# High weights against both parts of the activations in one 512-column matmul, and PSUM tiles left in two units

## The chip, the cores and the metric

The kernel runs on one core of a Trainium2 chip. The metric is the device time of one execution in microseconds (us); the figure for a kernel is the median over its runs. The engines are TensorE (PE; its weight loads are listed as PEld), VectorE (DVE), ScalarE (ACT), GpSimd (POOL) and SyncE (SP, which issues the DMAs).

## The reference, cut to what matters

The reference computes two transformer-like layers on 256 tokens with width 2048, in float32: adaLN modulation, gated linear attention, latent attention, a SwiGLU feed-forward part of hidden width 5632, then pooling, memory attention, compressed and windowed sparse attention, and RMS norms between them. Nearly all of the arithmetic is products of the 256 activations' rows with weight matrices:

```python
p = h @ w_in                      # 2048 x (many parts)
y_gla = o @ gla_wo ; y_mla = o_m @ mla_wo
merged = sigmoid(p_ga) * y_gla + sigmoid(p_gb) * y_mla ; x = x + gate_m * (merged @ w_out)
g, u = split(h @ ffn_w_in) ; x = x + gate_f * ((silu(g) * u) @ ffn_w_down)
# second layer: pool_u, pool_zu, nsa_k*, nsa_q, nsa_zq ... and two output products
```

## The kernel before, in words

**A split product.** Both factors are float32, and both are cut in two float32r parts: hi is the value as float32r holds it, lo is what is left. A product is hi·hi + hi·lo + lo·hi. The activations lie in SBUF with features on the partitions (h_hi, h_lo and the like: 128 partitions, 16 chunks, 256 tokens).

**Pieces and tiles.** A product (class `Product`, table `PRODUCTS`, L133 to L194) is a row of tiles, each 512 output features wide, and a tile is a row of kp pieces (kp is 4 for most, 6 and 5 in the two ffn_down products). A piece is 4 chunks of 128 input features by 512 output features, 1 MB, brought by one DMA into one of four buffers w_raw. Then ACT writes w_hi in two halves of 128x1024 (L1242), DVE writes w_lo in two halves (L1555); w_hi and w_lo have two buffers each, so the cut of piece n+2 waits until PE is done with piece n (semaphore piece_done).

**PE.** In `product` (L837 to L891) each piece waits for its w_lo; then, for each chunk, three passes (w_hi with x_hi, w_lo with x_hi, w_hi with x_lo) over four blocks of 128 output features: 48 matmuls of 256 columns, each with its own weight load. A few products have the weights as the moving operand instead (mode "N", 512 columns, gla_v for one; mode "R" for cmp_k1 and cmp_v1, where three matmuls in a row add into the same PSUM columns). A tile's sums, 4 blocks of 256 columns, fill one of the two buffers tile_ps[0], tile_ps[1] (two PSUM banks each), and the tiles take turns.

**Leaving PSUM.** After the last piece of a tile, one engine takes the whole tile of 128x1024: ACT with a copy, sigmoid or silu (`copy_to` L1285, `silu_g` L1455, `silu_gate` L1485) or DVE (`gated` L1910 to L1916, `gla_merge` L1924, `both_merge` L1950 to L1952, `add` in `residual` L1973 and L1977, `up` L1999 to L2005). In the program of ACT and of DVE (L1255 to L1271 and L1571 to L1590) the order is: the cuts up to the first piece of the next tile, with the steps of `between` after each of them, then the take of the tile, then the cut of the next tile's second piece. That last cut can begin only when the tile is done, so it lies behind the take, on both engines, while PE runs one piece. The PE waits again at that next tile's second piece.

**Other work on the same engines.** Products with a rider carry the adaLN product: after every second piece an extra 1 MB lands in w_raw, which DVE multiplies and adds in four steps of 128x512 (`ada_piece`, L1605, L1612), and PE sums it (`ada_total`, L893). `between` weaves in rotations, the log-sigmoid of gla_k (L1423 to L1425), the high part of z (L1511) and attention steps. `residual` products that feed a norm also square x on ACT (L1348) and, from the second tile on, reduce the squares on DVE (L1966).

**Loops.** `turns` (L625) makes a hardware loop of two tiles per turn for gate_a, gla_wo, mla_wo and the ffn_in products (L600 to L621 hold the waits with a loop count in them); the other split products are written out flat.

## Time and profile before

| | |
|---|---|
| median of 3 runs (lowest, highest) | 3026.41 us (3026.32, 3032.33) |
| the profiled execution | 3026.54 us, of it the span of the instructions 3024.7 us |
| PE busy / weight loads busy | 2817.4 us (93%) / 2703.1 us (89%) |
| DVE busy / ACT busy | 1830.7 us (61%) / 1195.1 us (40%) |
| mean granted TensorE clock | 0.969 |
| HBM read | 561.95 MB, 187 GB/s over the span |

The busy time of PE is the union of its matmuls, which overlap; the distance between two starts is what a matmul costs in a stream. A timeline row gives the start, the time until the end of the last of its instructions, the group and its count; in brackets stands the idle time before it and what ended it.

### The profile page before, as it was taken

To read this page: it belongs to the slowest core of one execution; us is meant where nothing else is said; L and a number is where in the kernel's file an instruction comes from. 1 tells how busy PE (TensorE), PEld (TensorE's weight loads), DVE (VectorE), ACT (ScalarE), POOL (GpSimd) and SP (SyncE) were. 2 spreads that over 40 slices of the span, in tenths; PEclk is the share of its full clock that TensorE was granted. 3 is DMA by queue.
4 is the path that set the end of the run, shared out by engine and by line. 5 is a ranking of instruction groups with operands and counts; after the bars stand their busy time and mean duration, and the time that the engine had idled before them with its cause. 6 is when DMAs were issued, how large, how long until landed. Compare 5 with 4: busy or idle time off the path is not lost.

```text
span 3024.7 us, 50507 instructions
## 1 busy us (share of the span) xinstructions
PE 2817.4 (93%) x21461; PEld 2703.1 (89%) x21461; DVE 1830.7 (61%) x2283; ACT 1195.1 (40%) x1508; POOL 5.6 (0%) x14
## 2 busy tenths in 40 slices
PE   3879988999999999989999999998998989899998
PEld 2879867999999779989999999997998989799887
DVE  7795666867665557774444444455566656646765
ACT  3435433343343433343333333333444434544543
POOL 0000000000000000000000000000000000000000
PEclk7989999999999989999999999999999999999998
DMA  7786831777777337745555555553554445665232
GB/s 266 280 313 220 288 111 70 257 258 274 250 241 216 91 109 254 265 166 194 180 180 181 181 181 181 180 180 125 168 181 157 162 148 181 199 184 164 87 106 88
DMA packets 319760, 568.44 MB, mean 188 GB/s; under 512 B 21962, under 2 KB 61218, under 8 KB 318963
## 3 DMA queue, kind: packets, MB, share of 16 engines
q1 hardware_dynamic: 318354, 561.73, 55.5%
q0 software_dynamic: 1248, 4.46, 0.4%
q8 instruction: 118, 1.93, 0.3%
q14 instruction: 40, 0.32, 0.0%
HBM read 561.95 MB, written 4.19 MB: 187 GB/s over the span
## 4 chain that ended last, share of the span: by engine, by line
PE 83%; DVE 12%; issue 2%; ACT 2%; DMA 1%; SPq 0%; DVEq 0%; ACTq 0%
PE tile_ps L835 75%; PE misc_ps L835 6%; DVE w_lo L1555 4%; DVE probs_t L1612 1%; ACT w_hi L1242 1%; PE misc_ps L977 1%; DVE rstd L1662 0%; DVE o_tmp L1999 0%; DVE x L1977 0%; DVE tile_ps L1895 0%; DVE gla_att L1898 0%; DMA w_raw<-in_w_mem_kv 0%; PE tile_ps L1017 0%; DVE stats L1774 0%; DMA mem_rows<-in_mem 0%
## 5 line engine op out<-in xcount | busy, mean ns | idle before, releaser
L1555 DVE TENSOR_TENSOR w_lo<-w_raw,w_hi 128x1024 fp32r<-128x1024 f32 x866 | 1021.8, 1222 | 885.5 <-ACT w_hi L1242 884.5
L1242 ACT ACTIVATE w_hi<-w_raw 128x1024 fp32r<-128x1024 f32 x866 | 867.9, 1050 | 1128.0 <-PE tile_ps L835 1086.5
L835 PE MATMUL tile_ps<-h_hi,w_hi 128*128 128x256 f32 x4208 | 697.0, 287 | 55.6 <-DVE w_lo L1555 34.6
L835 PE MATMUL tile_ps<-h_hi,w_lo 128*128 128x256 f32 x4208 | 687.0, 285 | 0.0
L835 PE MATMUL tile_ps<-h_lo,w_hi 128*128 128x256 f32 x4208 | 686.9, 285 | 0.0
L835 PEld LDWEIGHTS tile_ps<-h_hi,w_hi 128*128 128x128 f32 x4208 | 590.7, 194 | 65.3 <-issue 34.9
L835 PEld LDWEIGHTS tile_ps<-h_hi,w_lo 128*128 128x128 f32 x4208 | 587.9, 194 | 0.0
L835 PEld LDWEIGHTS tile_ps<-h_lo,w_hi 128*128 128x128 f32 x4208 | 587.7, 194 | 0.0
L1612 DVE SCALAR_TENSOR_TENSOR probs_t<-w_raw,c_act,probs_t 128x512 f32<-128x512 f32 x360 | 270.3, 751 | 10.9
L835 PE MATMUL tile_ps<-o_hi,w_hi 128*128 128x256 f32 x1024 | 168.4, 287 | 14.4 <-DVE o_lo L1648 6.9
L835 PE MATMUL tile_ps<-o_hi,w_lo 128*128 128x256 f32 x1024 | 165.9, 285 | 0.0
L835 PE MATMUL tile_ps<-o_lo,w_hi 128*128 128x256 f32 x1024 | 165.5, 284 | 0.0
L835 PEld LDWEIGHTS tile_ps<-o_hi,w_hi 128*128 128x128 f32 x1024 | 142.7, 194 | 16.3 <-issue 11.4
L835 PEld LDWEIGHTS tile_ps<-o_hi,w_lo 128*128 128x128 f32 x1024 | 142.6, 194 | 0.0
L835 PEld LDWEIGHTS tile_ps<-o_lo,w_hi 128*128 128x128 f32 x1024 | 142.2, 193 | 0.0
L835 PE MATMUL tile_ps<-sw_hi,w_hi 128*128 128x256 f32 x704 | 113.8, 284 | 1.7 <-DVE w_lo L1555 1.5
L835 PE MATMUL tile_ps<-sw_hi,w_lo 128*128 128x256 f32 x704 | 113.3, 283 | 0.0
L835 PE MATMUL tile_ps<-sw_lo,w_hi 128*128 128x256 f32 x704 | 113.3, 283 | 0.0
L835 PEld LDWEIGHTS tile_ps<-sw_hi,w_hi 128*128 128x128 f32 x704 | 97.1, 192 | 2.7 <-DVE w_lo L1555 2.7
L835 PEld LDWEIGHTS tile_ps<-sw_lo,w_hi 128*128 128x128 f32 x704 | 97.2, 192 | 0.0
L835 PEld LDWEIGHTS tile_ps<-sw_hi,w_lo 128*128 128x128 f32 x704 | 97.2, 192 | 0.0
L835 PE MATMUL tile_ps<-w_hi,h_hi 128*128 128x512 f32 x224 | 70.7, 397 | 0.0
(330 smaller groups left out, 2281.3 us busy)
## 6 DMA issues: line engine op xcount, KB each, us to landing
w_raw<-in_ada_w SPq DMA_DIRECT2D x96, 1024.0 KB, 5.2
w_raw<-in_w_in SPq DMA_DIRECT2D x89, 1024.0 KB, 5.1
w_raw<-in_ffn_w_in SPq DMA_DIRECT2D x88, 1024.0 KB, 5.0
w_raw<-in_w_out SPq DMA_DIRECT2D x48, 1024.0 KB, 5.1
w_raw<-in_ffn_w_down SPq DMA_DIRECT2D x44, 1024.0 KB, 5.1
w_raw<-in_b_w_in SPq DMA_DIRECT2D x33, 1024.0 KB, 5.3
w_raw<-in_a_w_in SPq DMA_DIRECT2D x32, 1024.0 KB, 5.6
w_raw<-in_w_kv SPq DMA_DIRECT2D x24, 1024.0 KB, 5.1
```

The source lines that it names most:

```text
L835: return nc.tensor.matmul(o, l, r, start=start, stop=stop, skip_group_check=True)
L977: last = nc.tensor.transpose(bank[2][0:k, a * P:(a + 1) * P], probs_of(name, u0 + e)[:, hd * nk + j * P:hd * nk + j * P + k], ident)
L1242: f(w_hi[s_ % 2][:, hf], w_raw[r % 4][:, hf], ACT.Copy).then_inc(cut_hi, 1)
L1555: ins = v.tensor_tensor(w_lo[s_ % 2][:, hf], w_raw[r % 4][:, hf], f32(w_hi[s_ % 2][:, hf]), ALU.subtract)
L1612: ins = v.scalar_tensor_tensor(acc, w[:, c, :], c_act[:, k:k + 1], acc, ALU.mult, ALU.add)
```

## The change

- `Product.paired` holds for split products of mode "T" with at least four pieces per tile, other than pool_out, nsa_out, mem_k0, mem_k1, nsa_qm and nsa_zm. Such a tile is two units (nu = 2) of two blocks of 128 output features. A unit has its own tile_ps buffer: each block fills one bank of 512 columns.
- The hi and lo part of an activation lie in one tensor (h_2, o_2, cq_2, ckv_2, sw_2). For each chunk and block PE runs one matmul of 512 columns, w_hi with the 256 columns of x_hi and the 256 of x_lo, and one of 256 columns, w_lo with x_hi, into the first half of the same bank. A piece runs unit 0's four chunks, then unit 1's. The first tile after a norm (`by_chunk`) goes chunk by chunk instead, except in its last piece.
- Unit 0 is done half a piece before the tile (semaphore half_done). Where `folds` holds (all paired products but w_out, ffn_down0, ffn_down1), each unit leaves PSUM so: ACT copies the second halves of both banks (128x512) into `folded`, a part of probs_t; DVE adds the first halves and frees the PSUM buffer; the former take follows, at 128x512, from SBUF; it raises `made`, and the next unit's ACT copy waits for it, since there is one `folded`.
- The residual products add the two halves to x one after the other on DVE, eight steps of 128x256 for a tile where there were four.
- In ACT's and DVE's programs a `between` step that followed the cut of the next tile's first piece now follows the two takes.
- The two accumulators of the adaLN product become one in mla_ckv (`ada_turns`).

The core of the diff:

```diff
+        self.paired = kp >= 4 and split and mode == "T" and not late and name not in ONE_BY_ONE
+        self.folds = self.paired and name not in RESIDUAL
+        self.nu = 2 if self.paired else 1
...
-        h_hi = at("h_hi", HB, [P, DC, S], F32R)
-        h_lo = at("h_lo", HB + 16 * KB, [P, DC, S], F32R)
+        h_2 = at("h_2", HB, [P, 2, DC, S], F32R)
+        h_hi, h_lo = h_2[:, 0], h_2[:, 1]
...
+        folded = probs_t[:, 1, :].rearrange("p (a n) -> p a n", a=2)
...
+        def sums_from(ps, h):
+
+            return ps[:].rearrange("p (a b n) -> p b a n", a=2, b=2)[:, h]
...
+                        def two_blocks(u, c):
                             k = q * g.kc + c
...
+                            ps = psum_unit(g, g.nu * tb + u)[0]
+                            for j in range(2):
+                                at_ = slice((2 * u + j) * P, (2 * u + j + 1) * P)
+                                mm(ps[:, j * 512:j * 512 + 512], w[0][:, c, at_], x_2(tb, k), k == 0, False)
+                                last = mm(ps[:, j * 512:j * 512 + S], w[1][:, c, at_], x_hi(tb, k), False,
+                                          k == g.kp * g.kc - 1)
+                            return last
...
+                        elif g.paired:
+                            for u in range(2):
+                                unit_is_free(u)
+                                for c in range(g.kc):
+                                    if u == 0:
+                                        chunk_is_there(c)
+                                    last = two_blocks(u, c)
+                                if u == 0 and q == g.kp - 1:
+                                    last.then_inc(half_done, 1)
...
-                                do_next(between)
-                        if take:
-                            ps, tk = psum_tile(g, tb)
-                            tile_is_done(act, g, i, tb)
-                            take(i, tb, g, ps, tk)
+                                if not (g.paired and e == g.done_at[tb]):
+                                    do_next(between)
+                        for u in range(g.nu * tb, g.nu * tb + g.nu):
+                            ps, tk = psum_unit(g, u)
+                            if g.folds:
+                                low_part(i, u, g, ps)
+                            if take:
+                                unit_is_there(act, g, i, u)
+                                take(i, u, g, ps, tk)
+                        if g.paired:
+                            do_next(between)
+
+            def low_part(i, u, g, ps):
+
+                unit_is_done(act, g, i, u)
+                unit_is_made(act, g, i, u - 1)
+                f(folded, sums_from(ps, 1), ACT.Copy).then_inc(low_out, 1)
...
+            def fold(i, u, g, ps, tk):
+
+                dve.wait_ge(low_out, g.f0 + u + 1 + per(i, g.body * g.nu))
+                v.tensor_tensor(folded, sums_from(ps, 0), folded, ALU.add).then_inc(tk, 1)
...
-            def both_merge(i, tb, g, ps, tk):
-                tile_is_done(dve, g, i, tb)
-                last_taken(dve, g, i, tb)
-                t = in_chunks(mla_tmp[:])
-                step(i, tb, g, 0, v.tensor_tensor(t, in_chunks(ps[:]), some(gate_b, i, tb, g), ALU.mult))
-                step(i, tb, g, 1, v.tensor_tensor(t, t, some(merged, i, tb, g), ALU.add))
-                split_to(i, tb, g, 2, t, some(h_hi, i, tb, g), some(h_lo, i, tb, g), tk)
+            def both_merge(i, u, g, ps, tk):
+                unit_is_taken(dve, g, i, u)
+                step(i, u, g, 0, v.tensor_tensor(folded, folded, some(gate_b, i, u, g), ALU.mult))
+                step(i, u, g, 1, v.tensor_tensor(folded, folded, some(merged, i, u, g), ALU.add))
+                split_to(i, u, g, 2, folded, some(h_hi, i, u, g), some(h_lo, i, u, g), made)
...
-                    for c in range(BLK):
-                        cc = (i * g.body + tb) * BLK + c
-                        ins = v.scalar_tensor_tensor(x[:, cc, :], ps[:, c * S:(c + 1) * S], mod[:, part * DC + cc:part * DC + cc + 1],
-                                                     x[:, cc, :], ALU.mult, ALU.add)
+                    for h in range(2):
+                        for c in range(2):
+                            cc = (i * g.body * 2 + u) * 2 + c
+                            ins = v.scalar_tensor_tensor(x[:, cc, :], sums_from(ps, h)[:, c, :], mod[:, gate * DC + cc:gate * DC + cc + 1],
+                                                         x[:, cc, :], ALU.mult, ALU.add)
+                        if h == 0:
+                            own.wait(ins)
...
-                t = o_tmp[:, 0, :]
...
-                v.tensor_tensor(t, ps[:], t, ALU.mult).then_inc(tile_step, 1)
...
+                unit_is_taken(dve, g, i, u)
+                silu = in_pair(o_tmp[:, 0, u % 2 * 512:u % 2 * 512 + 512])
+                m = u // 4 * 2 + u % 2
+                step(i, m, g, 0, v.tensor_tensor(folded, folded, silu, ALU.mult))
+                at_ = bass.ds(per(i, g.body * 2) + 2 * m, 2)
+                split_to(i, m, g, 1, folded, sw_hi[:, at_, :], sw_lo[:, at_, :], made)
```

## Rows read from the trace of the kernel before

**Rows 1.** The page: busy time of each engine.

```profile
PE 2817.4 (93%) x21461; PEld 2703.1 (89%) x21461; DVE 1830.7 (61%) x2283; ACT 1195.1 (40%) x1508; POOL 5.6 (0%) x14
```

**Rows 2.** The page: the chain that ended last, by engine and by line.

```profile
PE 83%; DVE 12%; issue 2%; ACT 2%; DMA 1%; SPq 0%; DVEq 0%; ACTq 0%
PE tile_ps L835 75%; PE misc_ps L835 6%; DVE w_lo L1555 4%; DVE probs_t L1612 1%; ACT w_hi L1242 1%; PE misc_ps L977 1%; DVE rstd L1662 0%; DVE o_tmp L1999 0%; DVE x L1977 0%; DVE tile_ps L1895 0%; DVE gla_att L1898 0%; DMA w_raw<-in_w_mem_kv 0%; PE tile_ps L1017 0%; DVE stats L1774 0%; DMA mem_rows<-in_mem 0%
```

**Rows 3.** Waits, whole span: in total us, times, longest us.

```profile
PE tile_ps L835 <- DVE w_lo L1555: 54.7, 28, 15.4
```

**Rows 4.** Busy time by stretch: gate_a (a rider), and pool_zu to pool_zm.

```profile
604.00:698.90 94.90, 94.70 (x788) 94.09 (x786) 63.29 (x67) 41.14 (x40) 0.00 (x0) 1.00 0.76 266
2190.00:2305.00 115.00, 115.00 (x961) 115.00 (x960) 63.72 (x57) 48.69 (x47) 0.00 (x0) 1.00 0.52 167
```

**Rows 5.** Timeline of PE, ffn_in0: start us, us, group.

```profile
1500.40 0.64 PE L835 MATMUL tile_ps<-h_hi,w_lo 128*128 128x256 f32 x4
1500.88 0.64 PE L835 MATMUL tile_ps<-h_lo,w_hi 128*128 128x256 f32 x4
```

**Rows 6.** Timeline of PE, gla_v: matmuls of 512 columns.

```profile
340.36 0.61 PE L835 MATMUL tile_ps<-w_hi,h_hi 128*128 128x512 f32 x2
340.81 0.62 PE L835 MATMUL tile_ps<-w_lo,h_hi 128*128 128x512 f32 x2
```

**Rows 7.** Timeline of PE, cmp_k1: each adds into the same PSUM columns.

```profile
2594.12 0.28 PE L835 MATMUL tile_ps<-w_lo,z_hi 128*60 128x256 f32 x1
2594.24 0.28 PE L835 MATMUL tile_ps<-w_hi,z_lo 128*60 128x256 f32 x1
```

**Rows 8.** Timeline of ACT and DVE at a tile's end in ffn_in0, silu tile.

```profile
1346.64 1.03 ACT L1485 ACTIVATE o_tmp<-tile_ps 128x1024 f32<-128x1024 f32 x1 [2.39 <-PE tile_ps L835]
1347.56 1.99 ACT L1242 ACTIVATE w_hi<-w_raw 128x1024 fp32r<-128x1024 f32 x2
1348.64 2.36 DVE L1555 TENSOR_TENSOR w_lo<-w_raw,w_hi 128x1024 fp32r<-128x1024 f32 x2 [4.18 <-ACT w_hi L1242]
```

**Rows 9.** Timeline at a tile's end in ffn_down1: DVE's cut and PE's wait.

```profile
2005.15 2.36 DVE L1555 TENSOR_TENSOR w_lo<-w_raw,w_hi 128x1024 fp32r<-128x1024 f32 x2 [2.14 <-ACT w_hi L1242]
2006.43 0.64 PE L835 MATMUL tile_ps<-sw_lo,w_hi 128*128 128x256 f32 x4
2007.57 0.39 PE L835 MATMUL tile_ps<-sw_hi,w_hi 128*128 128x256 f32 x1 [0.49 <-DVE w_lo L1555]
```

**Rows 10.** Groups by form: operations of 128x512 (and 128x256 for L1977).

```profile
L1363 ACT ACTIVATE probs_t<-misc_ps 128x512 f32<-128x512 f32 x28 | 16.7, 597 | 59.7 <-PE misc_ps L977 59.7
L1770 DVE SCALAR_TENSOR_TENSOR probs<-misc_ps,const 128x512 f32<-128x512 f32 x6 | 4.1, 686 | 6.0 <-PE misc_ps L835 4.9 <-PE misc_ps L977 1.1
L1977 DVE SCALAR_TENSOR_TENSOR x<-tile_ps,mod,x 128x256 f32<-128x256 f32 x48 | 19.9, 478 | 27.2 <-PE tile_ps L835 27.2
```

**Rows 11.** Timeline of DVE, the looped up tile of ffn_in0.

```profile
1415.92 1.23 DVE L1999 TENSOR_TENSOR o_tmp<-tile_ps,o_tmp 128x1024 f32<-128x1024 f32 x1 [2.40 <-PE tile_ps L835]
1417.31 0.69 DVE L2003 CAST sw_hi<-o_tmp 128x1024 f32 x1 [0.16 <-DVE o_tmp L1999]
1419.27 2.35 DVE L1555 TENSOR_TENSOR w_lo<-w_raw,w_hi 128x1024 fp32r<-128x1024 f32 x2
```

**Rows 12.** PE's waits in two windows: gla_g (527:604), mla_wo (1112:1212.9).

```profile
PE tile_ps L835 <- DVE w_lo L1555: 1.9, 2, 0.9
...
PE tile_ps L835 <- DVE w_lo L1555: 3.8, 3, 1.6
```

**Rows 13.** Timeline of ACT: a table load in gate_a, the log-sigmoid of gla_k.

```profile
284.47 0.58 ACT L1423 ACTIVATE log_a<-misc_ps 128x512 f32<-128x512 f32 x1
288.31 0.63 ACT L1425 ACTIVATE log_a<-log_a 128x512 f32<-128x512 f32 x1
...
628.37 1.28 ACT L1285 ACT_TABLE_LOAD   x1 [3.83 <-PE tile_ps L835]
```

**Rows 14.** Groups by form: the high part of z.

```profile
L1511 ACT ACTIVATE z_hi<-z_pe 128x1920 fp32r<-128x1920 f32 x2 | 3.6, 1794 | 0.0
```

More of the change, by code:

```diff
@@ L130, in constants @@
     return c, g.reshape(P, GLA_CONST_W)
+RESIDUAL = ("w_out", "ffn_down0", "ffn_down1")
+ONE_BY_ONE = ("mem_k0", "mem_k1", "nsa_qm", "nsa_zm")
 class Product:
@@ L220 @@
         _s += _g.tiles * _g.kp * _g.split
-        _t += _g.tiles
+        _t += _g.tiles * _g.nu
+        _f += _g.tiles * _g.nu * _g.folds
+        _h += _g.tiles * _g.paired
     _a += _g.ada_tiles(_g.tiles)
@@ L251 @@
     _k += _g.sums != "shared"
-    _a += {"pairs": _g.n // 2, "tiles": 4, "shared": 0, "heads": GLA_H}[_g.sums]
+    _a += {"pairs": _g.n // 2, "tiles": 4 * _g.nu, "shared": 0, "heads": GLA_H}[_g.sums]
     _m += {"pairs": _g.n // 2, "tiles": 1, "shared": 0, "heads": 1}[_g.sums]
@@ L601, in all_taken @@
         def all_taken(eng, g):
+            if g.folds:
+                eng.wait_ge(made, g.f0 + g.tiles * g.nu)
+                return
             for b in range(2):
@@ new lines, in unit_is_free, with chunk_is_there @@
+                        def unit_is_free(u):
+                            use = (g.t0 + g.nu * tb + u) // 2
+                            if use and q == 0:
+                                pe.wait_ge(psum_unit(g, g.nu * tb + u)[1], use + per(i, g.body * g.nu // 2))
+                        def chunk_is_there(c):
+                            if tb == 0 and chunk_ready:
+                                for sem_, v_ in chunk_ready(q * g.kc + c):
+                                    pe.wait_ge(sem_, v_)
@@ L1117, in _ @@
             product("gate_a", *h)
-            for b in range(2):
-                pe.wait_ge(taken[b], (G["gla_g"].t1 - b + 1) // 2)
+            all_taken(pe, G["gla_g"])
             product("gla_wo", *o)
@@ L1459, in _ @@
             product("gla_wo")
[L1460 to L1461 removed]
+            product("mla_cq", copy_to(chunks(cq), pre=[(piece_done, G["gla_wo"].p1)]))
+            product("mla_ckv", copy_to(chunks(ckv)))
             all_taken(act, G["mla_cq"])
             norm("cq")
[L1464 removed]
+            product("mla_kr", copy_to(lambda i, u, g: k_rope[:, :]))
             all_taken(act, G["mla_ckv"])
             norm("ckv")
[L1467 removed]
+            product("gate_b", copy_to(chunks(gate_b), ACT.Sigmoid, pre=[(made, G["gla_g"].f0 + G["gla_g"].tiles * 2)]), flat=True)
             for hf in range(2):
                 free = [(piece_done, G["gate_b"].p1)] if hf == 0 else [(at_o, U0["mla0"] + len(UNITS["mla0"]))]
[L1470 to L1473 removed]
+                product(f"mla_qn{hf}", copy_to(chunks(mla_q), pre=free))
+                product(f"mla_qr{hf}", copy_to(chunks(mla_qr)))
+                product(f"mla_k{hf}", copy_to(chunks(mla_k)))
+                product(f"mla_v{hf}", copy_to(columns(mla_v)))
                 attention(f"mla{hf}")
@@ L1479, in silu_gate, with take @@
             def silu_gate(part):
-                def take(i, tb, g, ps, tk):
-                    if tb % 2:
-                        return
-                    act.wait_ge(taken[(g.t0 + 1) % 2], (g.t0 + 1 + tb) // 2 + per(i, g.body // 2))
-                    f(o_tmp[:, 0, :], ps[:], ACT.Silu).then_inc(tk, 1)
+                def take(i, u, g, ps, tk):
+                    if u // 2 % 2 == 0:
+                        f(in_pair(o_tmp[:, 0, u % 2 * 512:u % 2 * 512 + 512]), folded, ACT.Silu).then_inc(made, 1)
                 return take
@@ L1586, in product @@
                                     cut(g, i, g.s0 + e, g.p0 + e, ring_of(g, e))
-                                do_next(between)
-                        if take:
-                            ps, tk = psum_tile(g, tb)
-                            take(i, tb, g, ps, tk)
+                                if not (g.paired and e == g.done_at[tb]):
+                                    do_next(between)
+                        for u in range(g.nu * tb, g.nu * tb + g.nu):
+                            ps, tk = psum_unit(g, u)
+                            if g.folds:
+                                fold(i, u, g, ps, tk)
+                            if take:
+                                take(i, u, g, ps, tk)
+                        if g.paired:
+                            do_next(between)
+            def fold(i, u, g, ps, tk):
+                dve.wait_ge(low_out, g.f0 + u + 1 + per(i, g.body * g.nu))
+                v.tensor_tensor(folded, sums_from(ps, 0), folded, ALU.add).then_inc(tk, 1)
             def ada_piece(g, i, tb, q):
```

309 lines of the change are left out of this document (160 added, 149 removed).

## The prediction

> **What bounds the kernel now.** First the busy times: PE works 93% of the span, its weight loads 89%, DVE 61%, ACT 40% [rows 1]. Then the chain that ended last: 83% of it is PE, 75% the split products; the only other entry of size is DVE's w_lo with 4% [rows 2]. The waits say the same: PE stands 54.7 us in all for w_lo, in 28 places [rows 3]. The busy times by stretch show how full PE is: in pool_zu to pool_zm it never idles, 961 matmuls in 115.0 us, 0.120 us each; in gate_a it nearly never does, with the DMA engines at 0.76 and 266 GB/s [rows 4]. So a gain must come from PE's stream, and a loss from what ends after PE: the second piece of a tile, whose w_lo lies behind the taking of the tile before.
>
> **PE's stream.** Two groups of four 256-column matmuls start 0.48 us apart, 0.120 each [rows 5]; two groups of two 512-column matmuls 0.45 to 0.46, 0.227 each over a stretch (1340.36 to 1344.44 in such rows is 18 matmuls in 4.08 us) [rows 6]. So 256 columns more cost 0.107, and each matmul has a fixed 0.013 with its weight load. Before, a chunk and block cost 3 x 0.120 = 0.360; after, 0.227 + 0.120 = 0.347. The columns streamed, 768, stay; only one fixed part goes. A piece of 16 such pairs goes from 5.76 to 5.55, 0.208 less. Paired are 78 tiles: 70 of 4 pieces, 4 of 6 and 4 of 5, which is 324 pieces: **-67.4 us** in all. Nine of these pieces start a stage and last as long as a norm or the attention before them: +1.9.
>
> The trace has no 512 beside a 256 and none whose moving operand is two runs of 256. In cmp_k1 matmuls of 256 columns that add into the same PSUM columns start 0.12 apart [rows 7], so adding to what was just written costs nothing. Bounds for the pair: 0.321 (columns alone, 3 x 0.107) and 0.360 (the fixed part comes back). I take 0.347, the sum of the two nearest rows.
>
> The Trainium skill, "TensorE: Matmul & The Clock Gate", section "Wait — 56ns, not 53.3ns?", gives N/2.4 GHz plus about 2.5 ns between matmuls, 216 ns for 512 columns, and has weight loads run ahead. By it the pair would be about 325 ns and the saving 180 us by an estimate. The rows here show 227 and 120, so the trace disagrees.
>
> **The drain.** PE loses time at a tile's second piece when w_lo's second half ends later than 0.32 before the end of the running piece: in ffn_down1 it ends at 2007.51, 0.44 after the piece (2006.43 + 0.64), PE restarts at 2007.57, and an unhindered stream would have restarted 0.16 before the piece's end, with 0.11 for refilling [rows 9]. I count T from the tile's end on PE; the next piece then has until T + 5.76 - 0.32 = 5.44 before, T + 5.23 after.
>
> Before, an ACT tile: copy starts at T+0.04, w_hi 0.92 later, first half 1.05, w_lo 0.03 later, 2.36 for both halves: 4.4 [rows 8]. No loss.
>
> After, unit 1 is the one that counts. Operations at 128x512: ACT 0.60, DVE 0.69 [rows 10]. Handovers between engines are 0.03 to 0.09 in flat code [rows 8], 0.16 in loops [rows 11].
> - **ACT tile, flat** (28: gla_q, gla_k, mla_cq, mla_ckv, gate_b, pool_u to pool_zm, nsa_kc, vc, ks, kw, q, zq): 0.07 + 0.60 + 0.03 + 0.69 + 0.06 + 0.53 (copy until w_hi may start) + 1.05 + 0.03 + 2.36 = 5.42, loss 0.2: +5.6. Unit 0 costs nothing: its sums are there at T-2.7, DVE is through with its w_lo at T-2.0, so it is folded by T-1.3. If that cover is gone, its 1.9 us join the 5.42.
> - **gate_a** (4, loop): 5.6, loss 0.4. Before, two loop turns lost some 0.3 per tile behind a table load of 1.28 [rows 13], which now falls beside unit 0: +1.
> - **gla_wo** (4): take is one multiply, ACT cuts meanwhile: w_lo ends at 4.6, no loss.
> - **ffn_in** (11 pairs of silu and up tile, loop): the silu tile loses 0.4. In the up tile DVE folds, multiplies, casts (0.43, an estimate from 0.69 at 1024) and subtracts: 0.84 + 0.84 + 0.56 + 0.60 = 2.84. Unit 0 starts it at T-2.0 and is made at T+1.0; only then may ACT copy unit 1: 1.1 to 1.7, fold at 1.8, w_lo starts at 4.6 and ends at 7.0. Loss 1.75. Before, w_lo ended at 1419.27 + 2.35, with DVE's take from 1415.92 on [rows 11]: loss 0.4. Difference 1.75: +19.3. That is all the 18.3 that their 88 pieces save.
> - **mla_wo** (4, loop): one operation more per unit: unit 0 is made at T+1.8, w_lo ends at 8.6, loss 3.4; before 1.8 (idle 1.6 and refill) [rows 12]: +6.4.
> - **gla_g** (4, flat): two steps of 0.48, multiply, cast, subtract: made at T+1.5, w_lo ends at 7.8, loss 2.6; before 1.2 [rows 12]: +5.6.
> - **w_out, ffn_down** (12): four steps of 0.478 [rows 10] and one wait more for unit 1 (1.9 against 1.7), a square of half the size on ACT: the loss of 0.76 in w_out and ffn_down1 grows by 0.1, ffn_down0 loses nothing: +0.6.
> - **between moved behind the takes.** DVE's steps lie beside ACT's copy and w_hi: nothing. ACT's do not: one log-sigmoid of gla_k, 4.5 us from 284.47 to 288.94 [rows 13], makes that loss 4.7, with a window of 1.2 gone elsewhere, and the other three windows stay bound by ACT: +4.1. The high part of z in nsa_ks, 1.79 [rows 14]: +1.9.
> - **Stage ends.** Where a later stage waits for the last unit, 1.0 later, mostly hidden: +1.5. The riders' adaLN steps on DVE end just in time before their piece's w_lo; SP's DMAs are the same in number and order, and 266 GB/s becomes 276: nothing. The queues that wait behind `made` are ACT's cuts, counted above. POOL has no step in it.
>
> **Sum:** -67.4 + 1.9 + 5.6 + 1 + 19.3 + 6.4 + 5.6 + 0.6 + 4.1 + 1.9 + 1.5 = **-19.5 us**. The profiled execution took 3026.5 (span 3024.7), the median is 3026.4: **3007 us**.
>
> **The rivals.**
> 1. *The drain is longer than I count* (slower). Place: the handovers ACT, DVE, ACT of unit 1 between T and the next w_lo. Price: 78 tiles; 0.25 us more in each and no gain is left. If every flat handover costs the loop's 0.16 to 0.24, five of them add 0.6 in some 40 flat tiles (24 us) and 0.3 in the others (11 us): 3042. For: five steps follow one another with nothing beside them. Against: the flat rows agree on 0.03 to 0.09.
> 2. *The pair costs 0.360*: the second run of the operand, or the change of length, brings the 0.013 back. Drains stay at +48: 3074. For: no row shows such an operand. Against: the fixed part is the same at 256 and 512.
> 3. *Columns alone count*: if the fixed part comes from a weight load that the 256-column stream is too short for, the 512 makes room, and the pair costs 0.321. Then a piece is 5.14, the pieces save 201 us, and the drains lose 0.4 more in some 60 tiles: about 2898. Against: 512 in a row cost 0.227, not 0.214 [rows 6]. The rule of the Trainium skill's "TensorE: Matmul & The Clock Gate" quoted above leads here.
> 4. *Nothing of note*: drains eat the saving to within the measurement. It is the upper part of my own case.
>
> **How the numbers follow.** What a measurement of this kernel can tell from no change is 0.2%, 6 us. My case has 0.75: 2985 to 3025, of it 0.66 faster, 0.09 same. Rival 1 has 0.15 (0.12 slower, 0.03 same), rival 2 0.05, rival 3 0.03, and 0.02 for no change at all. Together faster 0.69, same 0.14, slower 0.17. The range that leaves out 2 in 10 goes from 2980 (ACT and DVE steps overlap more than counted) to 3038.
>
> **What would show it.** In the changed profile the 512- and 256-column matmuls should start 0.347 us apart per pair and a flat stretch such as pool_zu should take 5.55 per piece; PE's waits for w_lo should grow from 54.7 to some 90 us, most of it in ffn_in and mla_wo, at second pieces; in an up tile ACT's copy of unit 1 should start about 1 us after T. The prediction is wrong if pairs start 0.36 or 0.32 apart, if ffn_in's stretch of 12 tiles changes by more than 5 us, or if flat ACT tiles lose more than 0.5 each.

## The result, and the profile after

The changed kernel took 3039.88 us (median of 20 runs, 3030.86 to 3051.89), the kernel before, on the same chip, 3028.3 us (20 runs, 3022.92 to 3032.4). The ratio is 1.0042, 95% interval 1.0032 to 1.0053: **slower by 0.4%**, where 0.6% faster was forecast. The profiled execution of the changed kernel took 3051.07 us (span 3049.3), one of its longest.

The page of the changed kernel: busy times, the chain by engine and by line, and three groups (the drain's two new operations and the 512-column matmuls; the number behind the bar is busy us and mean ns, then the idle time before).

```profile
PE 2806.6 (92%) x16277; PEld 2439.1 (80%) x16277; DVE 1950.0 (64%) x2528; ACT 1286.1 (42%) x1695; POOL 5.6 (0%) x14
...
PE 79%; DVE 13%; ACT 3%; issue 3%; DMA 1%; SPq 0%; DVEq 0%; ACTq 0%
...
L878 PE MATMUL tile_ps<-h,w_hi 128*128 128x512 f32 (+1 forms) x4448 | 1502.8, 391 | 79.1 <-DVE w_lo L1644 47.9
...
L1690 DVE TENSOR_TENSOR probs_t<-tile_ps,probs_t 128x512 f32<-128x512 f32 x132 | 91.2, 691 | 114.3 <-ACT probs_t L1360 112.2
...
L1360 ACT ACTIVATE probs_t<-tile_ps 128x512 f32<-128x512 f32 x132 | 79.1, 599 | 152.8 <-PE tile_ps L878 97.1
```

There are 5184 matmuls fewer than in [rows 1], yet PE is busy only 10.8 us less, and PE's share of the chain is 79% where [rows 2] had 83%. The stream did become cheaper; the time came back as waits, and as PE time at half clock. The waits of PE, whole span (us in total, times, longest):

```profile
PE tile_ps L878 <- DVE w_lo L1644: 69.2, 37, 15.4
...
PE tile_ps L878 <- issue: 15.8, 7, 4.2
```

The first row answers to [rows 3]. The second is new: five of its seven waits stand at tile starts of ffn_in0 (below).

**Where it went, product by product.** The table sets the time from the end of one product to the end of the next, read off PE's last matmuls in both traces, against the prediction's terms shared out over the products (0.208 us per piece, and the drain's terms).

| product | pieces | forecast, us | measured, us |
|---|---|---|---|
| gla_k (log-sigmoids moved) | 8 | +2.8 | +2.4 |
| gla_g | 16 | +2.3 | +7.9 |
| gate_a | 16 | -2.3 | +2.7 |
| gla_wo | 16 | -3.3 | -3.4 |
| mla_cq, mla_ckv, mla_kr | 8 | at most +0.2 | +4.7 |
| mla_qn0, mla_qn1 (attention beside them) | 0 | 0 | +11.9 |
| mla_wo | 16 | +3.1 | +4.5 |
| w_out | 16 | -3.1 | +0.1 |
| ffn_in0 | 48 | +0.5 | +8.6 |
| ffn_in1 | 40 | +0.4 | -0.1 |
| ffn_down0, ffn_down1 | 44 | -8.9 | -3.4 |
| pool_u to pool_zm | 32 | -5.1 | -2.6 |
| nsa_kc to nsa_kw | 16 | -0.6 | -0.5 |
| nsa_q, nsa_zq | 24 | -3.8 | -4.1 |

The measured column, with gla_q, gate_b and what little lies in the rest, makes the 24.6 us between the two spans. Five things carry the miss: ffn_in0, the attention stage, a group of products with one or two pieces of 9.2 to 9.7 us (gla_g, gate_a, mla_wo, w_out), mla_kr, and a stream that in most pieces is slower than forecast, which shows best in the ffn_down products, where little else changed. The busy times of four stretches, after (the stretch and its length, busy us and instructions of PE, PEld, DVE, ACT and POOL, then the granted clock, the DMA share and GB/s, as in [rows 4]):

```profile
401.90:611.20 209.30, 181.63 (x964) 147.33 (x962) 146.28 (x167) 70.63 (x75) 0.00 (x0) 0.94 0.34 121
...
846.10:860.40 14.30, 11.19 (x63) 10.15 (x63) 6.76 (x12) 6.98 (x12) 0.00 (x0) 0.76 0.44 159
...
1335.20:1636.20 301.00, 281.42 (x1558) 242.34 (x1559) 167.65 (x191) 128.66 (x152) 0.00 (x0) 0.97 0.48 167
1773.10:2004.90 231.80, 227.80 (x1281) 196.04 (x1281) 124.51 (x129) 97.60 (x109) 0.00 (x0) 1.00 0.53 181
```

These are gla_g, mla_kr, ffn_in0 and ffn_in1. In ffn_in0 PE idles 19.6 us, in ffn_in1, which does the same work on ten tiles, only 4.0.

**The stream.** PE's 512-column matmuls after, one pair with its neighbour in pool_zu:

```profile
2231.11 0.40 PE L878 MATMUL tile_ps<-h,w_hi 128*128 128x512 f32 x1
2231.35 0.28 PE L878 MATMUL tile_ps<-h,w_lo 128*128 128x256 f32 x1
2231.46 0.40 PE L878 MATMUL tile_ps<-h,w_hi 128*128 128x512 f32 x1
```

The 512 takes 0.24, the 256 behind it 0.11. Over longer stretches there are two rates: in gla_wo 17 pairs in 5.89 us (729.95 to 735.84), 0.347 each as forecast; in ffn_in1 15 pairs in 5.30 us (1818.27 to 1823.57), 0.353. A piece is so 5.55 or 5.65; of the 324 pieces 94 have the first, 143 the second, and 12 lie between 5.70 and 5.80. A piece keeps the rate of the one before it as long as nothing is waited for: among neighbours at one of the two rates it is the same in 150 of 152 cases.

**The drain, as it was counted.** ffn_in1, silu and up tile: what ACT and DVE do around the end of an up tile, and where PE restarts.

```profile
1819.23 0.60 ACT L1360 ACTIVATE probs_t<-tile_ps 128x512 f32<-128x512 f32 x1 [2.90 <-DVE sw L1750]
...
1819.86 0.69 DVE L1690 TENSOR_TENSOR probs_t<-tile_ps,probs_t 128x512 f32<-128x512 f32 x1 [0.67 <-ACT probs_t L1360]
...
1820.66 0.69 DVE L2099 TENSOR_TENSOR probs_t<-probs_t,o_tmp 128x512 f32<-128x512 f32 x1
...
1821.51 0.43 DVE L1749 CAST sw<-probs_t 128x512 f32 x1 [0.16 <-DVE probs_t L2099]
...
1822.08 0.69 DVE L1750 TENSOR_TENSOR sw<-probs_t,sw 128x512 f32 x1
...
1822.69 2.35 DVE L1644 TENSOR_TENSOR w_lo<-w_raw,w_hi 128x1024 fp32r<-128x1024 f32 x2
...
1825.10 0.51 PE L878 MATMUL tile_ps<-h,w_hi 128*128 128x512 f32 x1 [1.01 <-DVE w_lo L1644]
```

The first row waits 2.90 us for unit 0 to be made (the one buffer folded), and unit 1's four operations then follow one another on DVE. The second piece of the tile that follows an up tile takes 6.91 to 6.93, a loss of 1.26, where 1.75 was forecast.

**ffn_in0.** The same operations around 1395.8, where an up tile ends:

```profile
1393.65 0.69 DVE L1690 TENSOR_TENSOR probs_t<-tile_ps,probs_t 128x512 f32<-128x512 f32 x1
...
1395.56 0.69 DVE L1750 TENSOR_TENSOR sw<-probs_t,sw 128x512 fp32r<-128x512 f32 x1
...
1396.37 0.60 ACT L1360 ACTIVATE probs_t<-tile_ps 128x512 f32<-128x512 f32 x1 [2.75 <-DVE sw L1750]
...
1397.00 0.69 DVE L1690 TENSOR_TENSOR probs_t<-tile_ps,probs_t 128x512 f32<-128x512 f32 x1 [0.74 <-ACT probs_t L1360]
...
1397.79 0.47 PE L878 MATMUL tile_ps<-h,w_hi 128*128 128x512 f32 x1 [2.00 <-issue]
```

Here PE doesn't start the next silu tile at 1395.8. It stands 2.00 us, until 0.10 after unit 1 of the tile before has been folded. The page puts that down to "issue", but five such restarts, at 1397.79, 1446.74, 1494.11, 1543.09 and 1590.62, all come right behind a fold. The reason is in the program: `by_chunk` asks for both units' PSUM before the first chunk, in every tile with tb == 0, and in a hardware loop of two tiles per turn that is the first tile of every turn, not of the product alone. Unit 1's bank is then wanted as soon as PE ends the tile before, half a piece earlier than otherwise.

**The clock.** Windows over the 4 us behind three of the waits: one in gla_g (1.94 us before it), the first and the second of ffn_in0 (2.00 and 2.22 us before them):

```profile
541.50:545.50 4.00, 3.89 (x13) 3.36 (x14) 3.89 (x6) 0.28 (x1) 0.00 (x0) 0.57 0.67 217
1397.50:1401.50 4.00, 3.71 (x13) 3.19 (x14) 3.90 (x6) 2.00 (x2) 0.00 (x0) 0.61 0.13 51
...
1446.50:1450.50 4.00, 3.76 (x21) 3.33 (x22) 3.67 (x6) 2.01 (x2) 0.00 (x0) 1.00 0.05 17
```

In the first two PE issues 13 matmuls where it issues 21 in the third: the granted clock went from 2.4 to 1.2 GHz behind the wait. A piece of ffn_in0 that starts so takes 9.36 or 9.55, one that starts behind as long a wait at full clock 8.01 to 8.16: **1.2 to 1.5 us more**, on top of the wait. Beside gla_k's piece of 10.45, which waits for a log-sigmoid, ten paired pieces of the changed kernel take 9.16 to 10.51 us (three in gla_g, two in mla_wo and in ffn_in0, one each in gate_a, gate_b and w_out); the kernel before has two (10.14 in gla_g, 9.73 in gate_b). Summed from the clock's records between 100 and 2900 us of the span, it stands at 1.2 GHz for 201 us after and for 126 us before. Time and clock go together in the other runs as well: of the changed kernel's 20 runs the fastest (3030.86 us) has a mean clock of 0.964, the slowest (3051.89) 0.957.

**mla_kr.** ACT and DVE at the end of mla_ckv:

```profile
844.48 0.57 ACT L1360 ACTIVATE probs_t<-tile_ps 128x512 f32<-128x512 f32 x1
845.93 0.69 DVE L1690 TENSOR_TENSOR probs_t<-tile_ps,probs_t 128x512 f32<-128x512 f32 x1
...
846.65 0.63 ACT L1369 ACTIVATE ckv<-probs_t 128x512 f32<-128x512 f32 x1 [1.60 <-DVE probs_t L1690]
...
847.37 0.60 ACT L1360 ACTIVATE probs_t<-tile_ps 128x512 f32<-128x512 f32 x1
848.00 0.69 DVE L1690 TENSOR_TENSOR probs_t<-tile_ps,probs_t 128x512 f32<-128x512 f32 x1 [1.39 <-ACT probs_t L1360]
848.73 0.63 ACT L1369 ACTIVATE ckv<-probs_t 128x512 f32<-128x512 f32 x1 [0.76 <-DVE probs_t L1690]
849.26 1.13 ACT L1399 ACTIVATE nscratch_o<-cq 128x512 f32<-128x512 f32 x2
...
849.93 3.78 PE L878 MATMUL misc_ps<-nscratch_o,const 128*128 128x256 f32 x8 [3.07 <-ACT nscratch_o L1399]
```

The same sums in the kernel before:

```profile
841.42 2.00 PE L835 MATMUL misc_ps<-nscratch_o,const 128*128 128x256 f32 x8 [0.85 <-ACT nscratch_o L1307]
```

Unit 0's fold sits behind DVE's w_lo, unit 1's copy behind unit 0; ACT's program has the squares of cq, which were ready long before, behind all this. PE waits 3.07 us for them (before: 0.85), and its eight sums then take 3.78 us instead of 2.00, at half clock; over the stretch the mean clock is 0.76, where it was 1.00. Of the 4.9 us that mla_kr is longer 2.2 are so the wait and 1.8 the clock behind it.

### The profile page after: what moved, and what is told of

The parts are those of the page before. It is cut to its first block, busy times and chain, and to the rows that moved or that the text cites. A ratio compares the mean times of both kernels' runs of the same rounds, so it can differ in the third digit from the quotient of the medians.

```text
span 3049.3 us, 40930 instructions
## 1 busy us (share of the span) xinstructions
PE 2806.6 (92%) x16277; PEld 2439.1 (80%) x16277; DVE 1950.0 (64%) x2528; ACT 1286.1 (42%) x1695; POOL 5.6 (0%) x14
## 4 chain that ended last, share of the span: by engine, by line
PE 79%; DVE 13%; ACT 3%; issue 3%; DMA 1%; SPq 0%; DVEq 0%; ACTq 0%
PE tile_ps L878 72%; PE misc_ps L878 6%; DVE w_lo L1644 4%; DVE probs_t L1712 2%; ACT w_hi L1319 1%; DVE probs_t L1690 1%; ACT probs_t L1360 1%; PE misc_ps L1054 1%; DVE rstd L1764 0%; DVE x L2079 0%; DVE tile_ps L1997 0%; DVE gla_att L2000 0%; DVE part_o L2067 0%; DMA w_raw<-in_w_mem_kv 0%; DVE probs_t L2099 0%
## 5 line engine op out<-in xcount | busy, mean ns | idle before, releaser
L878 PE MATMUL tile_ps<-h,w_hi 128*128 128x512 f32 (+1 forms) x4448 | 1502.8, 391 | 79.1 <-DVE w_lo L1644 47.9
L878 PE MATMUL tile_ps<-h,w_lo 128*128 128x256 f32 x4208 | 1165.8, 283 | 0.0
L878 PEld LDWEIGHTS tile_ps<-h,w_hi 128*128 128x128 f32 x4448 | 824.3, 191 | 275.8 <-DVE w_lo L1644 58.0
L878 PEld LDWEIGHTS tile_ps<-h,w_lo 128*128 128x128 f32 x4208 | 797.5, 192 | 0.6
L878 PE MATMUL tile_ps<-o,w_hi 128*128 128x256 f32 (+1 forms) x1536 | 333.6, 325 | 17.7 <-DVE w_lo L1644 8.7
L878 PEld LDWEIGHTS tile_ps<-o,w_hi 128*128 128x128 f32 x1536 | 232.8, 193 | 43.9 <-DVE w_lo L1644 10.6
L878 PE MATMUL tile_ps<-sw,w_hi 128*128 128x512 f32 x704 | 249.1, 399 | 3.4 <-DVE w_lo L1644 3.4
L878 PE MATMUL tile_ps<-o,w_lo 128*128 128x256 f32 x1024 | 227.5, 283 | 0.0
L878 PE MATMUL tile_ps<-sw,w_lo 128*128 128x256 f32 x704 | 197.4, 280 | 0.0
L878 PEld LDWEIGHTS tile_ps<-o,w_lo 128*128 128x128 f32 x1024 | 170.0, 193 | 0.0
L878 PEld LDWEIGHTS tile_ps<-sw,w_hi 128*128 128x128 f32 x704 | 132.2, 188 | 37.6 <-DVE w_lo L1644 5.0
```

The source lines that it names most:

```text
L878: return nc.tensor.matmul(o, l, r, start=start, stop=stop, skip_group_check=True)
```

## The experiments

Ratios are to the kernel before on the same chip, with 95% intervals. All start from the changed kernel. The lengths of stretches come from one profiled execution each.

**1. No chunk order in ffn_in0.**

```diff
-            product("ffn_in0", *h, chunk_ready=as_normed("ffn"), by_chunk=True)
+            product("ffn_in0", *h, chunk_ready=as_normed("ffn"))
```

> The changed kernel with by_chunk taken from ffn_in0 alone. In the trace of the changed kernel PE stands 2.0 to 2.3 us at the start of five silu tiles of ffn_in0, until the fold of the up tile's second unit is done, and never so in ffn_in1. Theory A: by_chunk holds in every turn of PE's loop, since the turn's first tile is tb 0, and it asks for both units at once. Then these five waits go, waits of about 1.0 for w_lo at the second piece take their place as in ffn_in1, ffn_in0 falls from 301 us to about 293, and the ratio to the kernel before falls from 1.0042 by about 0.003 to 1.001. Rival B: the waits come from the drain itself, one folded buffer and made; then they stay or move, ffn_in0 stays at 299 to 302 and the ratio at 1.004.

Measured: 3034.98 us, 1.0035 (1.0021 to 1.0049). ffn_in0:

```profile
1324.80:1617.30 292.50, 279.35 (x1558) 240.13 (x1559) 167.53 (x191) 128.65 (x152) 0.00 (x0) 0.98 0.51 172
```

292.5 where it was 301.0, PE idle 13.1 instead of 19.6; the five waits at tile starts are gone and second pieces of 6.6 to 7.0 stand in their place, as in ffn_in1. The clause that `by_chunk` gives every turn costs 8.5 us in this stretch; 6.5 of them are idle time, and most of the rest is the clock, which fell behind two of the five waits and behind none here. The ratio shows less of it than was expected: it fell by 0.0007, not by 0.003, and the two intervals overlap. The fastest run fell from 3030.86 to 3025.32 us and the slowest from 3051.89 to 3044.46, so the medians agree with a gain, but the 8.5 us rest on the two profiles.

**2. No low copy.** ACT's copy and DVE's fold are replaced by one DVE copy of the first halves: the sum of w_hi with x_lo, in the second halves, is left out of the output.

```diff
-                                low_part(i, u, g, ps)
...
-                v.tensor_tensor(folded, sums_from(ps, 0), folded, ALU.add).then_inc(tk, 1)
+                v.tensor_copy(folded, sums_from(ps, 0)).then_inc(tk, 1)
```

> The changed kernel without ACT's copy of the second halves: DVE copies the first halves to folded and no lo-part sum is added, so the product of w_hi with the activations' lo part is left out. The drain of each folding unit is shorter by one ACT step and one handover, 0.6 to 0.7 us. Theory A (the drain between a tile's end and the next w_lo sets the loss): waits of PE for w_lo at second pieces shrink by about 0.65 in each of the some 35 tiles that lose now, twice that in ffn_in's up tiles and mla_wo where unit 0 hands on to unit 1, some 30 to 40 us in all, ratio about 0.992. Rival B (the drain costs little, the loss lies in PE's stream or in the clock): ratio stays within 0.002 of 1.0042.

Measured: 3013.97 us, 0.9957 (0.9940 to 0.9974). gla_g took 203.9, gate_a 93.3, mla_wo 141.8, w_out 94.2 (its late pieces without a clock fall), ffn_in0 294.8, ffn_in1 227.3, mla_kr 12.5. So one more operation of 0.60 us and its handover in each unit's way costs some 26 us (1.0042 less 0.9957, times 3026; 30 to 40 had been expected), and without it the change would be faster than before.

**3. Order of the matmuls.** Two 512-column matmuls, then the two of 256.

```diff
                             for j in range(2):
                                 at_ = slice((2 * u + j) * P, (2 * u + j + 1) * P)
                                 mm(ps[:, j * 512:j * 512 + 512], w[0][:, c, at_], x_2(tb, k), k == 0, False)
+                            for j in range(2):
+                                at_ = slice((2 * u + j) * P, (2 * u + j + 1) * P)
                                 last = mm(ps[:, j * 512:j * 512 + S], w[1][:, c, at_], x_hi(tb, k), False,
                                           k == g.kp * g.kc - 1)
```

> The changed kernel with another order in a unit's chunk: the two matmuls of 512 columns first, then the two of 256. In the changed kernel some pieces of 16 pairs take 5.55 us and others 5.65, with starts 117 and 230 ns apart in the first and 114, 232, 118, 240, 120, 236 in the others. Theory A (the swapping of lengths, 512 after 256 after 512, sets off the second pattern): pieces take 5.55 or less all over and the ratio falls by 0.003. Rival B (the pattern comes from how PE's clock edges fall when it restarts, whatever the order): both lengths of piece stay, ratio within 0.001 of 1.0042. Rival C: 512 columns behind 512 cost what gla_v shows, 0.227, and 256 behind 256 0.120, so 5.55 all over.

Measured: 3035.2 us, 1.0036 (1.0020 to 1.0051). PE in pool_zu:

```profile
2231.54 0.62 PE L878 MATMUL tile_ps<-h,w_hi 128*128 128x512 f32 x2
...
2232.23 0.63 PE L878 MATMUL tile_ps<-h,w_hi 128*128 128x512 f32 x2
```

0.69 to 0.70 for two pairs. 222 pieces now take 5.53 to 5.61 (5.57 most of them) and 11 take 5.61 to 5.70, where there were 94 and 143: the slower rate is all but gone. What it is worth follows from the counts: 143 pieces by 0.08 less 94 by 0.02, 10 us of PE time; ffn_in1 fell by 2.2 us. The ratio fell by 0.0006 only, so of the 10 us the times of whole runs show next to nothing; they spread over 19 us here.

**4. A filled wait.** 8 matmuls of 512 columns whose result nobody reads, ahead of the second piece of the odd tiles of gla_g and mla_wo, in the wait for w_lo.

```diff
+                        if name in ("gla_g", "mla_wo") and tb == 1 and q == 1:
+                            for n_ in range(8):
+                                mm(bank[2], x_2(0, 0)[:, 0, 0:P], x_2(0, n_), True, True)
```

> The changed kernel with eight matmuls of 512 columns into an unused bank ahead of PE's wait at the second piece of the turn's second tile, in gla_g and mla_wo: some 1.8 us of PE work where it stands 1.9 to 2.3. In the changed kernel the piece behind such a wait takes 9.3 instead of 5.55 + 2.2, and the granted clock in the 4 us behind it is 0.57. Theory A (the wait of about 2 us lets the clock fall to 1.2 GHz and the piece behind pays 1.6 us): the clock stays at full in these four places, their pieces take 7.6 to 8.0, each 1.3 to 1.7 less, gla_g and mla_wo lose 5 to 6 us together; ratio down by 0.002. Rival B (the clock falls for another reason or the extra matmuls delay the piece): pieces stay at 9.3 or grow, the ratio stays.

Measured: 3028.71 us, 1.0012 (1.0000 to 1.0024). The window over gla_g, and PE where the added matmuls run:

```profile
406.00:611.40 205.40, 181.56 (x980) 146.59 (x978) 146.39 (x167) 70.64 (x75) 0.00 (x0) 0.97 0.36 124
```

```profile
542.32 2.00 PE L878 MATMUL misc_ps<-h 128*128 128x512 f32 x8
...
544.37 0.50 PE L878 MATMUL tile_ps<-h,w_hi 128*128 128x512 f32 x1
```

PE starts the piece when it would have in any case, but at 2.4 GHz. The pieces went from 9.31 and 9.26 to 7.81 and 7.80 in gla_g, from 9.72 to 8.15 in mla_wo, gla_g from 209.3 to 205.4 us, its clock from 0.94 to 0.97. In the changed kernel and in experiments 1, 3, 5, 7 and 9, where nothing fills them, the clock fell behind the waits at these four places in 22 of 24 cases; here it fell in none. Work that does nothing made the kernel faster, and the clock's fall behind a wait of 2 us costs 1.5 to 1.6 us apiece. Not all of the gain is the filling's: in gla_g a third piece, which is not filled, went from 10.51 to 8.96, and in gate_a and w_out one piece each kept its clock as well.

**5. Loops written out.** gate_a, gla_wo, mla_wo, ffn_in0 and ffn_in1 flat on ACT and DVE.

```diff
-            product("gate_a", copy_to(chunks(merged), ACT.Sigmoid))
+            product("gate_a", copy_to(chunks(merged), ACT.Sigmoid), flat=True)
```

> The changed kernel with gate_a, gla_wo, mla_wo and the ffn_in products written out flat on ACT and DVE (PE keeps its loops). A control for the next run, and a test of the handovers: in loops they take 0.1 more, at some five places between a tile's end and the next w_lo. Theory A (handovers count one by one): the wait of an up tile, 1.0 us of idle PE, falls by about 0.4, ffn_in0 and ffn_in1 fall by some 4 us together, the ratio by 0.001 to 0.002 from 1.0042. Rival B: nothing changes.

Measured: 3028.91 us, 1.0006 (0.9995 to 1.0017). gate_a 92.9 (97.6), w_out 94.0 (96.5), ffn_in1 229.2 (231.8), ffn_in0 299.4 (301.0), mla_wo 145.0 (145.5): some 12 us in these, of the handovers of 0.16 in loops and of the clock in gate_a and w_out.

**6. The next cut first.** As 5, and on both engines unit 1 is taken only after the next tile's second piece has been cut.

```diff
-                            if take:
+                            if take and g.folds and u % 2:
+                                late.append(taking)
+                            elif take:
...
+                                while late:
+                                    late.pop()()
```

> Flat as the run before, and the take of a folding tile's second unit comes after the cut of the next tile's second piece on both engines; only ACT's copy and DVE's fold stay ahead of it. Theory A (the loss is the cut's place behind the whole drain): w_lo ends at T + 4.2 instead of up to T + 8, PE's waits for w_lo go in ffn_in, gate_a and the flat tiles, and shrink to below 1 us in gla_g and mla_wo, where unit 0's take still holds unit 1; with them goes the clock's fall. Ratio 0.985 to 0.990. Rival B (what PE loses is in its stream or in other stages): ratio above 0.997.

Measured: 3030.17 us, 1.0001 (0.9987 to 1.0016): missed. By stretch the idea works where nothing else stands in the way: ffn_in1 took 221.9 us with PE busy for all of it, ten under the changed kernel and the kernel before, and mla_wo 141.0. But ffn_in0 (299.4) kept its five waits for the fold of unit 1, each 2.0 to 2.1 us, and the clock fell behind three of them. gla_g didn't move, and the profile has the attention's low clock (next section). The runs spread from 3012.83 to 3034.28, and again by clock: the three fastest have 0.963 to 0.965, all others 0.956 to 0.958. In ffn_in1, where PE never waits, all 40 pieces take 5.55, in the old order of the matmuls: the slower rate of the stream goes with the waits too.

**7. The between work back where it was**, after the first piece's cut.

```diff
-                                if not (g.paired and e == g.done_at[tb]):
-                                    do_next(between)
+                                do_next(between)
...
-                        if g.paired:
-                            do_next(between)
```

> The changed kernel with the between steps where they were, straight after the cut of the next tile's first piece and ahead of the takes. In the changed kernel gla_k's tile end costs 10.45 for a piece of 5.55 (a log-sigmoid of 4.5 us on ACT) and nsa_vs' second piece 7.41 for 5.44 (the high part of z). Theory A: nsa_vs loses its 2.0, and gla_k's 4.9 falls to below 1.5, since the log-sigmoid then runs before the tile's end; together 4 to 6 us, ratio 0.0015 less than 1.0042. Rival B: the step delays the drain of unit 0 and with it unit 1, and the loss only moves: gla_k stays within 1.5 of its 53.5.

Measured: 3036.13 us, 1.0036 (1.0020 to 1.0051). gla_k 50.9 against 53.5 (before: 51.0), nsa_vs 22.1 against 23.7, nsa_kc 36.5 against 37.6: 5 us in all, below what the ratio can tell from the changed kernel's.

**8. All four mends at once** (1, 3, 6, and each between step behind the next cut).

> The cut ahead of the second unit's take (flat), no by_chunk in ffn_in0, between steps after the next cut, and the 512-column matmuls of a chunk ahead of the 256 (pieces of 5.57 all over). The sum of the parts: 324 pieces of 5.57 instead of 5.76 save 61; the drains' loss of the kernel before in the same products, some 15, goes as well; left are mla_kr's 4.5 and the ends. Theory A: 60 to 70 us faster than the kernel before, ratio 0.977 to 0.981. Rival B (one of the mends does not add to the others, or the clock falls more often elsewhere): ratio 0.985 to 0.995.

Measured: 3004.23 us, 0.9933 (0.9921 to 0.9946), 0.7% **faster** than before. ffn_in0 and ffn_in1:

```profile
1326.50:1608.60 282.10, 273.47 (x1560) 238.07 (x1559) 166.90 (x192) 127.72 (x152) 0.00 (x0) 0.99 0.53 179
1743.20:1966.10 222.90, 222.90 (x1281) 194.48 (x1281) 123.68 (x130) 96.65 (x109) 0.00 (x0) 1.00 0.57 188
```

With `by_chunk` gone the five waits for the fold are gone too: ffn_in0 is 10.3 us under the kernel before, ffn_in1 9.0; every piece but the first of ffn_in0 takes 5.57 or 5.58. The forecast of the combination was still too good: between work behind the cut made gla_k 57.0 (PE stood 4.63 us for log_a ahead of its next gate matmul, 2.01 in the changed kernel), and mla_kr and gla_g kept their waits.

**9. The squares of cq ahead of mla_ckv.**

```diff
-            product("mla_ckv", copy_to(chunks(ckv)))
             all_taken(act, G["mla_cq"])
+            for j in range(N["cq"].n // 2):
+                square_pair("cq", j)
+            product("mla_ckv", copy_to(chunks(ckv)))
             norm("cq")
```

> The changed kernel with ScalarE's squares of cq (two 128x512 Squares for the norm of cq) moved ahead of mla_ckv's pieces and drain; nothing else. In the changed kernel's trace PE stood 3.07 us before 849.93 because these squares queue behind ckv's drain, which goes ScalarE, VectorE, ScalarE twice over (844.48 to 849.36); the stretch of mla_kr took 14.3 us against 9.4 before. Theory A (the drain's trips hold up what is queued behind them): the squares are done by about 825, PE starts the norm's sums right at mla_ckv's end, the wait of about 3.1 us goes, the mla_kr stretch takes 10.5 to 11.5, and the low clock behind it (849, 7 us) is gone or shorter; the ratio to before falls from 1.0042 to about 1.003 (1.002 to 1.004). Rival B (the norm's reciprocal and scaling, queued on VectorE behind ckv's folds and cuts, end last): the wait only moves behind the sums and mla_kr takes 13.5 to 14.5. Part of the shift against before, about 10 us in either direction, can come from the clock in the attention stage, which differs between runs of one kernel; the stretch decides, not the ratio.

Measured: 3034.79 us, 1.0022 (1.0005 to 1.0040). The squares of cq, the end of PE's wait for them, and PE's wait for the squares of ckv:

```profile
827.69 1.16 ACT L1399 ACTIVATE nscratch_o<-cq 128x512 f32<-128x512 f32 x2
```

```profile
850.11 1.97 PE L878 MATMUL misc_ps<-nscratch_o,const 128*128 128x256 f32 x8
...
861.86 1.65 PE L878 MATMUL misc_ps<-nscratch_o,const 128*128 128x256 f32 x3 [4.04 <-ACT nscratch_o L1399]
```

PE goes on without a wait, mla_kr took 8.4 instead of 14.3; the next norm then waits 4.04 us where it waited 2.04, and gate_b took 102.9 instead of 100.2: 3.2 us are left of the 5.9. Theory A holds for the cause, and the wait partly moved.

**10. The best version:** as 8 and 9, gla_k's between work left where it was, and the filling of 4 ahead of the third piece, where the wait now is.

> All mends of the run before together (no by_chunk in ffn_in0, the five products' takes unrolled, the second unit's take and the between work after the next cut, the two 512-column matmuls ahead of the two 256-column ones), and three more: gla_k's between work stays where it was (its second tile's first piece took 14.18 us with it moved, 10.45 without), the squares of cq ahead of mla_ckv, and 8 matmuls of 512 columns, whose result nobody reads, ahead of the third piece of every odd tile in gla_g and mla_wo, where PE waits about 2 us for the cut and the clock falls. Theory A (waits and the clock they cost are what is left): gla_k 53, mla_kr 11, gla_g 204.5, mla_wo 139, the sum of these mends 3.8 + 3 + 3 + 1.5 = about 11 us on 3004.2: 2993, ratio 0.990 (0.988 to 0.992). Rival B (the mends only move the waits, as the combined kernel's did before): ratio 0.9925 to 0.994.

Measured: 2995.06 us, 0.9887 (0.9872 to 0.9902), 1.1% faster than before and the best of all. PE's waits for w_lo are now a little shorter in sum than in [rows 3] (54.7 us in 28 places):

```profile
PE tile_ps L878 <- DVE w_lo L1663: 52.5, 29, 15.4
```

gla_k took 53.2, gla_g 204.6, mla_kr 8.4, mla_wo 139.6.

## Why the prediction was wrong

**The stream: right in kind, 14 us too dear.** 0.347 per pair was forecast, 0.347 and 0.353 were measured; rivals 2 and 3 (0.360, 0.321) are out. With rival 3 goes, for this stream, the rule of the Trainium skill's "TensorE: Matmul & The Clock Gate", section "Wait — 56ns, not 53.3ns?": the prediction's estimate by it was 0.325 per pair, and the trace disagrees. The term of -67.4 us was too large by the 143 slower pieces, 0.1 us each: 14 us, more than any other single term was off. What sets the rate isn't explained; experiment 3 shows that it depends on the order of the matmuls, and experiment 6 that a stretch without waits has the faster one throughout. (The two gla_v times that the prediction quotes as 1340.36 and 1344.44 are 340.36 and 344.44; the 18 matmuls in 4.08 us are right.)

**The drain: its terms were nearly right where they could be read, and rather too dear.** gla_k, nsa_vs's late second piece, gla_wo, nsa_q and nsa_zq came out within a microsecond. In ffn_in1 the agreement (+0.4 forecast, -0.1 measured) is luck: the stream saved 4 us there instead of 8, as nearly all its pieces are slow ones, and the drains cost 4 instead of 9 ("loss 1.75" measured 1.26). In mla_wo "loss 3.4" is 2.5 where the clock stayed up. Rival 1, handovers that eat the gain, gave the right time (3042) by the wrong way: the handovers measured 0.03 to 0.16, as counted.

**The step that failed first: "ffn_in (11 pairs ...)".** It took both products for alike. The sentence on `by_chunk` was read as the first tile after a norm, and the condition is tb == 0 inside a loop turn. Nothing in the prediction asks when PE wants a PSUM unit back; "Unit 0 costs nothing" was checked for the cut and not for the bank. Experiment 1: 8.5 us, some 3 of them by the clock of the next point.

**The second: the clock was left out.** Each loss was priced as the wait alone. Experiment 4 shows that a wait of 2 us costs 1.5 to 1.6 more where the clock falls behind it. It fell behind eight of the twelve waits of 1.8 to 2.3 us ahead of paired pieces, in ffn_in0 behind two of five, so it is a chance per wait, and the sum has no term for it. The changed kernel has eight such pieces more than the kernel before, some 12 us by the 1.5 of experiment 4, most of them where gla_g, gate_a and mla_wo came out above their terms. "The loss of 0.76 in w_out grows by 0.1" became 3.2, as one of its second pieces took 9.35.

**The third: "Stage ends ... mostly hidden: +1.5".** In mla_kr alone it is 4.9, of which 1.8 are again the clock. The drain is not just later by one operation: unit 0's fold queues behind w_lo on DVE, and ACT's program has independent work of another product, the squares, behind it. Experiment 9 shows the cause; net it is worth 3.2 us.

**The attention stage, not forecast at all.** mla_qn1 with the attention beside it took 53.9 us (43.2 before). The same windows after, and in experiment 3:

```profile
1009.00:1033.00 24.00, 22.47 (x60) 13.21 (x58) 9.08 (x22) 7.00 (x20) 0.00 (x0) 0.58 0.15 44
```

```profile
1009.00:1033.00 24.00, 22.05 (x110) 14.44 (x110) 16.15 (x38) 10.46 (x36) 0.00 (x0) 1.00 0.11 31
```

The program is the same there, and so is the short wait ahead; in experiments 1, 3 and 4 the clock stayed up and the stretch took 44.2 or 44.3 us, in the others it fell for 20 us or more and the stretch took 53.8 to 58.1. This is a difference of about 10 us between executions of like kernels, and it fits the wide spread of the changed kernel's runs (21 us against 9.5). The kernel before may have such runs too, as 7 of its 20 lie at 3030.5 to 3032.4, but none of them was profiled; whether the change makes the fall more frequent stays open. Without this stage the profiles differ by 12.7 us. That is near the 11.6 between the medians, but no proof, as some of the changed kernel's runs hold the fall and some may not.

**The account, as an estimate from the profiles.** Forecast was -19.5 us, the profiles differ by +24.6, so 44 us are to be found: 14 of the stream, 12 of the clock behind waits, 12 of the attention stage, 5 to 6 of ffn_in0's waits beyond their clock, some 3 of mla_kr beyond the forecast of +1.5, less some 5 that the drains of ffn_in1 cost less. Of these the stream's two rates and the attention's clock have no known cause.

**The test named in the prediction** was good: it said that it would be wrong if ffn_in's stretch of 12 tiles changed by more than 5 us; it changed by 8.6. PE's waits for w_lo rose to 69.2, not to 90: a part stands under "issue" as waits for a PSUM bank.

**Where the expected gain is:** in experiment 10. It took 31.6 us less than the kernel before on its chip, and by the two ratios some 47 less than the changed one, with the same matmuls, in the order of experiment 3, but for 32 that fill waits, and the same operations in the drain. By the lengths of the pieces the stream saves some 53 us in the changed kernel (67.4 less 14) and 61 at 5.57 per piece; the change gave it back by the order of the steps on ACT and DVE, a PSUM bank asked for too early, and the clock behind the waits, and in experiment 10 half of it is still missing. The same mends weren't tried on the kernel before. It too loses time at second pieces (54.7 us of waits, [rows 3]), so how much of the 31.6 us is due to the wider matmuls and how much to the mends alone is not shown.

## What to carry to other kernels

When a drain gets longer, look at what is queued behind it rather than at its own length: the cut that the stream waits for next should go ahead of the drain, and independent work of another product should not stand behind it. Ask of each new sub-tile at which moment its buffer is wanted back, with the loop's own conditions (a "first tile" test inside a loop body is true once per turn). Price a wait of about 2 us on a full TensorE stream with the clock that may fall behind it, here half as much again or more.

## What the runs showed of the hardware

- The granted clock fell from 2.4 to 1.2 GHz behind eight of twelve waits of 1.8 to 2.3 us in a stream that was full before and after (window 541.50 to 545.50 at 0.57), and did not behind the others (1446.50 to 1450.50 at 1.00). At four places where it fell in 22 of 24 cases, filling the wait with matmuls kept it up in all four and saved 1.5 us where it had fallen.
- The same pair of matmuls, 512 and 256 columns, runs at 0.347 or 0.353 us per pair for whole pieces; with two of 512 ahead of two of 256 it is 0.348 in nearly all. The rate changed at waits: without one a piece had the rate of the piece before it in 150 of 152 cases.
- A matmul of 512 columns whose moving operand is two runs of 256, 16 chunks apart, costs no more than one run in the pieces at the faster rate: 0.347 less the 0.120 of [rows 5] is the 0.227 of [rows 6].
